# One core, two transformer blocks: three of each set's four weight sums move from VectorE to adding DMA transfers issued by GpSimd, and sixteen small loads move to a later place

## The reference, cut to what matters

```python
D_MODEL = 1024
SEQ = 256
D_FF_2 = 2816

def swiglu(x, wg, wu, wd):
    return (jax.nn.silu(x @ wg) * (x @ wu)) @ wd

    # first block, each of two layers
    h = rms_norm(x, g_ffn_pre[i])
    gu = h @ w_gate_up[i]
    f = (jax.nn.silu(gu[..., :D_FF]) * gu[..., D_FF:]) @ w_down[i]
    x = x + rms_norm(f, g_ffn_post[i])

    # second block, each of two layers
    x = x + 0.5 * swiglu(rmsnorm(x, ffn1_norm[l]), ffn1_wg[l], ffn1_wu[l], ffn1_wd[l])
    ...
    o_a = mla_mixer(h_a, cs_a, mla_q_norm[l], mla_kv_norm[l], mla_w_uq[l], mla_w_ukv[l])
    ...
    x = x + 0.5 * swiglu(rmsnorm(x, ffn2_norm[l]), ffn2_wg[l], ffn2_wu[l], ffn2_wd[l])
```

## Time and profile before

| | |
|---|---|
| median of 3 runs | 1578.75 us (1578.44 to 1578.83) |
| span of the profiled execution, first to last instruction | 1575.8 us |
| TensorE busy | 1548.6 us, 98% of the span |
| VectorE busy | 1331.5 us, 84% |
| ScalarE busy | 989.4 us, 63% |
| GpSimd busy | 93.4 us, 6% |
| granted TensorE clock | 0.998 of full speed |

### The profile page before, as it was taken

How to read it: one execution, slowest core, us unless ns; L and a number is a source line. 1 busy time by engine, 2 the same in 40 slices (tenths; PEclk the granted TensorE clock), 3 DMA queues, 4 the chain that set the end, 5 groups by cost and what they waited for, 6 DMA issues and landing times.

```text
span 1575.8 us, 21205 instructions
## 1 busy us (share of the span) xinstructions
PE 1548.6 (98%) x8276; PEld 1281.0 (81%) x8276; DVE 1331.5 (84%) x1438; ACT 989.4 (63%) x1382; POOL 93.4 (6%) x184
## 2 busy tenths in 40 slices
PE   9999999999999999999999999999999999999998
PEld 8778888877888887888877888888788877788886
DVE  6869999786999988999758599998899866789997
ACT  7756666675666665666558566665556556666564
POOL 1000000030000030000030000002000003000000
PEclk9999999999999999999999999999999999999999
DMA  8326663623665367563540365637555452074561
GB/s 292 133 81 241 240 214 108 203 83 130 241 240 190 107 194 249 211 239 112 183 134 2 110 241 211 230 118 237 194 213 213 134 186 81 2 240 162 212 214 54
DMA packets 150771, 270.84 MB, mean 172 GB/s; under 512 B 4968, under 2 KB 73824, under 8 KB 150672
## 3 DMA queue, kind: packets, MB, share of 16 engines
q1 hardware_dynamic: 147696, 261.87, 48.3%
q0 software_dynamic: 2544, 7.09, 1.7%
q10 hardware_dynamic: 432, 0.53, 0.1%
HBM read 268.42 MB, written 1.05 MB: 171 GB/s over the span
## 4 chain that ended last, share of the span: by engine, by line
PE 89%; DVE 5%; ACT 2%; DMA 2%; issue 1%; SPq 0%; POOL 0%; POOLq 0%; DVEq 0%; ACTq 0%
PE pair L2781 12%; PE bank L2657 8%; PE bank L2659 8%; PE bank L2658 8%; PE pair L2870 7%; PE pair L2874 7%; PE pair L2871 7%; PE pair L2785 6%; PE bank L2751 6%; PE bank L2724 3%; PE pair L3138 2%; DMA fold_raw<-in_ffn_wu 2%; PE bank L3189 1%; PE bank L3159 1%; PE pair L2657 1%
## 5 line engine op out<-in xcount | busy, mean ns | idle before, releaser
L1649 DVE TENSOR_TENSOR w_lo<-raw,w_hi 128x2048 fp32r<-128x2048 f32 (+2 forms) x185 | 419.5, 2276 | 61.4 <-ACT w_hi L1016 60.2
L1016 ACT ACTIVATE w_hi<-raw 128x2048 fp32r<-128x2048 f32 (+2 forms) x189 | 358.7, 1904 | 110.6 <-PE bank L2659 46.8
L1016 ACT ACTIVATE w_hi<-fold_raw 128x2048 fp32r<-128x2048 f32 x108 | 206.9, 1916 | 72.4 <-PE pair L2785 32.9
L1649 DVE TENSOR_TENSOR w_lo<-fold_raw,w_hi 128x2048 fp32r<-128x2048 f32 x108 | 246.0, 2288 | 1.5 <-ACT w_hi L1016 1.1
L2781 PE MATMUL pair<-xt,w_hi 128*128 128x512 f32 x912 | 221.7, 394 | 0.1
L2657 PE MATMUL bank<-w_hi,hid_hi 128*128 128x512 f32 x528 | 206.9, 392 | 1.5 <-DVE w_lo L1649 1.5
L2658 PE MATMUL bank<-w_hi,hid_lo 128*128 128x512 f32 x528 | 205.7, 390 | 0.0
L2659 PE MATMUL bank<-w_lo,hid_hi 128*128 128x512 f32 x528 | 205.6, 389 | 0.0
L2781 PEld LDWEIGHTS pair<-xt,w_hi 128*128 128x128 f32 x912 | 167.7, 188 | 33.3 <-issue 0.5
L2785 PEld LDWEIGHTS pair<-xt,w_lo 128*128 128x128 f32 x912 | 118.1, 191 | 5.2
L2785 PE MATMUL pair<-xt,w_lo 128*128 128x256 f32 x912 | 119.7, 283 | 0.0
(11 more groups left out here) (355 smaller groups left out, 2627.0 us busy)
## 6 DMA issues: line engine op xcount, KB each, us to landing
raw<-in_ffn_wd SPq DMA_DIRECT2D x44, 1024.0 KB, 5.1
fold_raw<-in_w_gate_up SPq DMA_DIRECT2D x24, 1024.0 KB, 9.0
fold_raw<-in_ffn_wg SPq DMA_DIRECT2D x24, 1024.0 KB, 9.1
fold_raw<-in_ffn_wu SPq DMA_DIRECT2D x24, 1024.0 KB, 8.0
raw<-in_w_down SPq DMA_DIRECT2D x22, 1024.0 KB, 5.0
raw<-in_w_in SPq DMA_DIRECT2D x21, 1024.0 KB, 5.2
raw<-in_w_gate_up SPq DMA_DIRECT2D x20, 1024.0 KB, 5.1
raw<-in_ffn_wg SPq DMA_DIRECT2D x20, 1024.0 KB, 5.4
```

Source lines behind the costliest of these rows:

```text
L1016: act.activation(w_hi[u % RING][:, 0:filled(u)], raw_of(u)[:, 0:filled(u)], ACT.Copy)\
L1649: dve.tensor_tensor(w_lo[s][:, 0:filled(u)], raw_of(u)[:, 0:filled(u)], w_hi[s][:, 0:filled(u)].bitcast(F32), ALU.subtract)\
```

## The change

In each of the 18 sets GpSimd now issues three transfers with an accumulating operation, which read the destination, add the source and write it back. They form a chain: `add_right` adds the right quarter, read from HBM once more, onto `UPPER` (place 5); `add_to_left` adds that `UPPER` onto `LEFT` (place 3); `add_to_lower` adds that `LEFT` onto `LOWER` (place 6). The three VectorE sums of the same names go. `RIGHT` is still loaded for its own product. GpSimd's list gets the nine transfers of a part behind the norm that opens it. In the parts f = 2 and f = 4 the sixteen small transfers move to between the first and the second adding transfer of the third set, and wait until TensorE has used the up unit of group 8.

```diff
+SUM_STEP = (1, 16, 16, 16)
...
                     fold_free(k, 3)
                     if k:
-                        sp.wait_ge(fold_made[FOUR_SUM], fold_index(f, k))
+                        sp.wait_ge(fold_made[FOUR_SUM], 16 * fold_index(f, k))
                     load_quarter(LEFT, quarter(wg, 0, 256 * FOLD_GROUPS[k][0]))
...
                 def load_right(k):
                     fold_free(k, 4)
-                    if k:
-                        sp.wait_ge(fold_made[RIGHT_SUM], fold_index(f, k))
-                        sp.wait_ge(fold_made[THREE_SUM], fold_index(f, k))
                     load_quarter(RIGHT, quarter(wu, 1, 256 * FOLD_GROUPS[k][0]))
...
+            def quarters(tile):
+                return fold_raw[tile][:, :].rearrange("p (c n) -> p c n", c=4)
+
+            def add_right(f, k):
+                _, _, wu, _, _ = ffns[f]
+                pool.wait_ge(fold_landed[UPPER], 16 * (fold_index(f, k) + 1))
+                pool.wait_ge(fold_made[UPPER_SUM], fold_index(f, k) + 1)
+                pool.dma_start(quarters(UPPER), quarter(wu, 1, 256 * FOLD_GROUPS[k][0]), accum_op=ALU.add)\
+                    .then_inc(fold_made[RIGHT_SUM], 16)
+
+            def add_to_left(f, k):
+                pool.wait_ge(fold_made[RIGHT_SUM], 16 * (fold_index(f, k) + 1))
+                pool.wait_ge(fold_made[UPPER_SUM], fold_index(f, k) + 1)
+                pool.wait_ge(lo_ready, ffns[f][0] + FOLD_AT[k][0] + 1)
+                pool.dma_start(quarters(LEFT), quarters(UPPER), accum_op=ALU.add)\
+                    .then_inc(fold_made[THREE_SUM], 16)
+
+            def add_to_lower(f, k):
+                pool.wait_ge(fold_made[THREE_SUM], 16 * (fold_index(f, k) + 1))
+                pool.wait_ge(lo_ready, ffns[f][0] + FOLD_AT[k][1] + 1)
+                pool.dma_start(quarters(LOWER), quarters(LEFT), accum_op=ALU.add)\
+                    .then_inc(fold_made[FOUR_SUM], 16)
+
+            def fold_sums(f, folds, steps=(0, 1, 2)):
+                for k in folds:
+                    for i in steps:
+                        (add_right, add_to_left, add_to_lower)[i](f, k)
...
                 norm(3 + 4 * l)
+                fold_sums(l, range(FOLDS))
                 norm_halves(4 + 4 * l)
...
                 norm(9 + 3 * l)
-                if l:
-                    pool.wait_ge(turned_lo.sem, turned_lo.at(("o2", 0, 7)))
-                else:
-                    pool.wait_ge(prep_ready.sem, prep_ready.at(("rows", ("ffn1", 0), 3)))
+                fold_sums(2 + 2 * l, (0, 1))
+                fold_sums(2 + 2 * l, (2,), (0,))
+                pool.wait_ge(unit_used, ffns[2 + 2 * l][0] + UP_AT[8] + 1)
...
+                fold_sums(2 + 2 * l, (2,), (1, 2))
                 norm(10 + 3 * l)
...
                 norm(11 + 3 * l)
+                fold_sums(3 + 2 * l, range(FOLDS))
...
-                    act.wait_ge(fold_made[FOLD_SUM[place]], fold_index(f, k) + 1)
+                    act.wait_ge(fold_made[FOLD_SUM[place]], SUM_STEP[FOLD_SUM[place]] * (fold_index(f, k) + 1))
...
-                def right_sum(k):
-                def three_sum(k):
-                def four_sum(k):
```

More of the change, by code:

```diff
@@ L1817, in upper_sum @@
                        .then_inc(fold_made[UPPER_SUM], 1)
-                def right_sum(k):
-                    landed(k, RIGHT)
-                    dve.wait_ge(fold_made[UPPER_SUM], fold_index(f, k) + 1)
-                    dve.tensor_tensor(fold_raw[UPPER][:, :], fold_raw[UPPER][:, :], fold_raw[RIGHT][:, :], ALU.add)\
-                       .then_inc(fold_made[RIGHT_SUM], 1)
-                def three_sum(k):
-                    u = u0 + FOLD_AT[k][2]
-                    landed(k, RIGHT)
-                    dve.wait_ge(fold_made[UPPER_SUM], fold_index(f, k) + 1)
-                    dve.wait_ge(lo_ready, u0 + FOLD_AT[k][0] + 1)
-                    dve.tensor_tensor(fold_raw[LEFT][:, :], raw_of(u)[:, :], fold_raw[RIGHT][:, :], ALU.add)\
-                       .then_inc(fold_made[THREE_SUM], 1)
-                def four_sum(k):
-                    landed(k, LOWER)
-                    dve.wait_ge(fold_made[THREE_SUM], fold_index(f, k) + 1)
-                    dve.wait_ge(lo_ready, u0 + FOLD_AT[k][1] + 1)
-                    dve.tensor_tensor(fold_raw[LOWER][:, :], fold_raw[LEFT][:, :], fold_raw[LOWER][:, :], ALU.add)\
-                       .then_inc(fold_made[FOUR_SUM], 1)
                 def products_done(k, slot):
@@ L1913, in ffn @@
                 add_cross(2)
-                three_sum(0)
                 hidden_rest(1)
@@ L1918, in ffn @@
                 split_lo(u0 + DOWN_AT[1])
-                right_sum(0)
                 add_up(2)
@@ L1923, in ffn @@
                 split_lo(u0 + FOLD_AT[0][3])
-                four_sum(0)
                 split_lo(u0 + FOLD_AT[0][4])
@@ L1942, in ffn @@
                 split_lo(u0 + FOLD_AT[1][0])
-                right_sum(1)
                 add_cross(5)
-                three_sum(1)
                 split_lo(u0 + FOLD_AT[1][1])
@@ L1952, in ffn @@
                 split_lo(u0 + FOLD_AT[1][3])
-                four_sum(1)
                 hidden_rest(5)
@@ L1971, in ffn @@
                 split_lo(u0 + FOLD_AT[2][0])
-                three_sum(2)
                 add_cross(8)
@@ L1978, in ffn @@
                 split_lo(u0 + DOWN_AT[7])
-                right_sum(2)
                 split_lo(u0 + FOLD_AT[2][2])
@@ L1982, in ffn @@
                 first_gate(2)
-                four_sum(2)
                 split_lo(u0 + FOLD_AT[2][4])
```

## The result

| | median, us | lowest to highest | runs | profiled execution, span |
|---|---|---|---|---|
| before | 1578.79 | 1578.44 to 1579.09 | 4 | 1575.8 |
| after | 1662.31 | 1660.26 to 1663.9 | 4 | 1661.7 |

The changed kernel is slower: 1.0531 times the time before, 95% interval 1.0516 to 1.0546. The prediction said 1576.0 us with a range up to 1630 us, so the likeliest case had the wrong sign, and the measured time lies above the range.

The account below looks back on a forecast made before the run. TensorE, busy 98% of the span, was taken as the bound. 1575.8 - 6.6 for waits won + 2 x 1.9 for late sets = 1573.0 us of span; with 2.9 us around it 1576.0 us, range 1571.8 to 1630 us.

Parts of the forecast that it names:

- T: The end of a set's `upper_sum`, from which ready times and deadlines count: 145.5, 191.3 and 236.7 us in f = 0.
- Waits that go: TensorE's waits in f = 2 and f = 4, 3.5 + 3.1 us, all counted as won: 6.6 us.
- Part 1: 54 sums leave VectorE, 123.4 us of its time; alone worth up to 2.2 us, only in f = 2 and f = 4.
- Part 3: Length of one adding transfer of 1 MB: 2.6 us fixed plus 2 x 2.65 us, 7.9 us.
- threshold of 8.2 us: Time per add from which first and second sets have used their 0.6 us of slack and the chain is late.
- Part 5: Chain against deadlines: place 3 fits by 0.6 us in first and second sets; third sets fit except in f = 2, 4.
- Part 4: Deadlines: place 3 by T + 17.0, 19.6, 21.7 and place 6 by T + 26.2, 28.0, 30.3 in first, second, third sets.
- Packet for packet, so small rows hardly slow: Where both queues had work they moved 271 and 280 packets; a 1 KB-row load beside an add costs 0.4 us.
- Sharing by time: Rival, 9%: queues share by time, so loads beside the second add cost up to 2.4 or 2.65 us; 1603 us.
- Small loads' set: Third sets of f = 2 and f = 4: second add behind sixteen small loads, T + 23.6 against T + 21.7, late 1.9 us.
- late in every set: Rival, 24%: place 3 waits for two chained adds with ScalarE's list behind it; 1605 us at 9 us per add, 1661 at 10.
- The estimate of 6.6 us: Length of one adding transfer from the skill's 32 GB/s for two engines: 4.0 us for 1 MB, so 6.6 us.

Follow-up runs that it names:

- Experiment 1: The kernel before with only the sixteen small loads moved late as in the change, all sums on VectorE (also written `e1_loads_late`): 1568.0 us, ratio 0.993.
- e10_apart: The changed kernel with the small loads behind each third set's last add, and `three_sum` back on VectorE between two unchained adding transfers: 1567.45 us, ratio 0.9931.
- experiment 7: The changed kernel with ten small matmuls into an unused bank ahead of the seventh product of each first set: 1653.42 us, ratio 1.0473.
- experiment 5: The changed kernel with the sixteen small loads behind the third adding transfer of the third set in f = 2 and f = 4: 1647.86 us, ratio 1.044.
- experiments 8 and 10: 8: small loads late as in the change, only the right pair's sum by transfer, other sums on VectorE: 1568.33 us, ratio 0.9934. 10: the kernel e10_apart.
- experiment 6: The changed kernel with two ScalarE copies moved ahead of roundings in first sets, and the small loads behind the third set's adds: 1636.65 us, ratio 1.0367.

## Why the prediction was wrong, point by point

The step that failed is the comparison of parts 4 and 5. Place 6 of the first sets was to be ready at T + 24.0 against a deadline of T + 26.2; it was ready at T + 28.3 against a deadline of T + 23.4. Of these 7.1 us the chain itself has 4.3 and the deadline 2.8. The mechanism that came true was named among the rivals, and put at 24%.

- **Waits that go** (the 6.6 us): right in cause, too small. Experiment 1 gave 10.8 us. Missing was the half clock behind a wait of 3 us, which the earlier trace rows alone doesn't show and a window of the clock at 616 us would have.
- **Part 1**, VectorE: predicted 1208 us busy, measured 1214.5 us; alone worth nothing. `e10_apart` takes two of the three sums from VectorE and gains 0.5 us on `e1_loads_late`, less than two runs differ.
- **Part 3**, the add: predicted 7.9 us, measured 8.4 us. For the plain transfer it had 5.2 us, and 4.5 us were measured between two tiles, 5.8 us from HBM. So the add costs 3.9 us more than a copy, and not 2.65. And the 7.9 us stood 0.3 us from its own threshold of 8.2 us, and its ends were 5.2 and 18.4 us; an error of 6% carried it over, and the 24% for that side was too little.
- **Part 5**, hand-overs: 0.1 us allowed; measured 0.5 us to the first issue (145.7 to 146.23) and 0.3 us to each further one (the add of 146.23 + 8.4 is landed at 154.6 and the next is issued at 154.96). With the adds' 2 x 0.5 us more that makes T + 17.7 in place of T + 16.4, though the 0.4 us for loads beside the second add didn't come.
- **Part 4**, the deadlines of the first sets. I took T + 17.0 for place 3 of the first set, from the copy of the first product alone. In ScalarE's order `fifth_out` stands behind places 4 and 5 as well, 7.0 us from the start of place 3 to the end of `fifth_out` (163.41 to 170.42). The third product, which needs that copy, began at T + 22.9 in the kernel before (T there is 145.5), so place 3 is due at T + 15.9. For place 6 I took the product of place 6 itself, T + 26.2. `second_out` stands behind it, 2.4 us from the start of place 6 to the end of the copy (173.97 to 176.37), and the seventh product needs that at T + 25.8: due at T + 23.4. (My expectations for the experiments have T + 15.4 and 2.4 us late for place 3; read off these rows it is T + 15.9 and 1.8 us.) Both are the list in the program's text; I had read which product a place feeds, and not what stands behind it. The chain's own forecast for place 6, T + 24.0 to 24.4, would already have been late by this. TensorE before, first matmul of the third and of the seventh product:

```profile
168.47 0.44 PE L2870 MATMUL pair<-w_hi,xs_hi 128*128 128x512 f32 x1
...
171.31 0.40 PE L2870 MATMUL pair<-w_hi,xs_hi 128*128 128x512 f32 x1
```

- **Part 5**, the third add: counted as the other two. It landed after 10.3 us in the first set, and even without the add it took 9.1 us. "Packet for packet, so small rows hardly slow", read off a window of part 2, doesn't hold in this place: for some 3 us no row of the add moved while rows of SP's two loads did. Sharing by time, the rival of 9%, is not what happened either. So place 6 came at T + 28.3 against T + 23.4, and the seventh product starts at T + 30.7 (176.42) instead of T + 25.8. With about 1.5 us of half clock behind it (experiment 7) that is most of the 8.2 us of a first set.
- **Part 5**, second and third sets: place 3 came at T + 19.0 in the second set of part 0 (217.09 us), exactly as forecast, and at T + 20.2 in the third (267.09 us), inside its deadline of T + 21.7. Place 6 didn't: T + 29.8 against T + 28.0, and T + 31.1 against T + 30.3, behind third adds of 10.6 us. And behind its split on VectorE stands that of the next `down` unit, for which TensorE waits 1.0 us in each (the ten waits of 10.0 us above). The second sets and the third ones of parts 0, 1, 3 and 5 have 20.4 of the 94 us.
- **Small loads' set**: predicted late by 1.9 us, measured a wait of 9.1 us and 12.4 us of lag. The order was right, second add behind sixteen small ones in one queue. The sum had 10.7 + 7.6 + 5.3; measured are 11.1 + 14.0 + 5.9 = T + 31.0, at which place 3 was ready. The term that was mis-sized is the middle one, the drain: the small ones alone kept the engines for 9.4 us, and rows of other transfers moved among theirs (experiment 5).
- **Sums of rivals**: "late in every set" was the mechanism that came true, with 24%. Its table gave 1661 us, but for an add of 10 us; at the measured 8.4 us it gives less than 1605 us. That the number is met is chance: the add was overcounted, and the lateness that follows from it was undercounted.
- **The Trainium skill**, Collectives: The Full Stack, section "The bandwidth ceiling: the fold count and why AG ≠ RS ≠ AR", has an add at half the pace of a copy because it needs two reads. The runs agree in kind: 20.5% against 11.7% of the engines for the same bytes, 8.4 against 4.5 us. The estimate of 6.6 us worked out from its figure was 1.8 us too low.
- **Right**: none of the large waits above is for a load of SP; GpSimd's waits hold up nothing at the part's end; no idle VectorE ahead of `upper_sum` in part 2 after.

Open is why place 6 comes between T + 28.3 and T + 29.3 in the first sets of one kernel, and why rows of the two queues alternate in the earlier trace rows and not ahead of the third add. The 3 us of SP's loads are read from traces; no run moved those loads alone.

## What to carry to other kernels

Before putting a slow step into a chain, write down for the tile that it makes every instruction that stands behind the tile's reader on each engine, and take the earliest of their deadlines; here that was 1.1 and 2.8 us tighter than the deadlines that I had taken, more than the slack. Look, too, at what other queues have already issued when each step of the chain is due: here loads of another engine added 3 us to the third. One or two adding transfers cost nothing where each has a slack of more than its own 8.4 us (experiments 8 and 10), and three in a chain cost 80 us (experiment 5 against 1); a forecast whose slack is smaller than the uncertainty of its longest term should give the late case at least half. And look in the trace at the clock behind each wait: one of 3 us cost another 1.5 us or so.

## What the runs showed of the hardware

- An adding transfer of 1 MB between two tiles took 8.4 us from issue to landing, a plain one 4.5 us, and the queue's share of the engines rose from 11.7% to 20.5% for the same bytes.
- GpSimd's issue of one took 0.85 to 1.30 us with the add (the three rows of after) against 0.53 and 0.76 us for the same transfers plain:

```profile
L952 POOL DMA_DIRECT2D fold_raw<-fold_raw x18: 527/528/534, 157.4 to 1524.0; - x18
L937 POOL DMA_DIRECT2D fold_raw<-in_ffn_wu x12: 761/763/861, 607.2 to 1512.7; - x12
```

- An adding transfer of 1 MB behind sixteen small ones (2.17 MB) in one queue took 19.6 us from issue to landing in place of 8.4 us. Its first rows moved 7.3 us after its issue, 4.9 us before the last packet of the small ones.
- An adding transfer issued while another queue had large loads under way began 3.5 to 4.9 us after its issue (16 transfers) and landed after 10.2 to 11.6 us; two issued without such loads began after 1.4 us and landed after 7.1 us.
- Each short wait of TensorE cost about 0.3 us beyond the length that the wait view gives (experiment 6).
- After a wait of 2.91 us TensorE ran at 1.2 GHz (half of full) for 3.4 us; with small matmuls during the wait it stayed at 2.4 GHz.
